# Token groups of two, three and three blocks, with the second group's front spread over the pairs of two blocks

## The chip, the core and the metric

The kernel runs on one core of one Trainium2 chip. The metric is device time in microseconds (us) of one execution; lower is better. Three runs of the kernel before gave 3722.76, 3727.45 and 3729.0 us, median 3727.45.

## The reference, cut to what matters

One step of a hybrid decoder layer for 1024 prompt tokens and 8 sample tokens, all in float32, model width 1024.

```python
n = rmsnorm(x, g_mix) * (1 + sc1) + sh1            # sc, sh, gt come from silu(c) @ w_ada + b_ada
z = n @ w_in                                       # 1024 -> 4096: a_lin, a_gate, u, v, g_a, g_b
a = silu(layernorm(causal_dwconv(a_lin * sigmoid(a_gate)))) @ w_conv_out      # 31 taps
b = (u * chunk_spatial_gate(layernorm(v))) @ w_gmlp_out                       # chunks of 128 tokens
x = x + gt1 * ((sigmoid(g_a) * a + sigmoid(g_b) * b) @ w_out)
n2 = rmsnorm(x, g_ffn) * (1 + sc2) + sh2
# PEER, per token: q = n2 @ w_q (8 heads x 2 halves), scores against 128 keys each,
# top 16 of both halves, top 16 of their sums -> 8 x 16 = 128 experts out of 16384
act = gelu(u_tab[eid] . n2);  x = x + gt2 * sum(softmax_weight * act * v_tab[eid])
y = rmsnorm(x, g_final)
```

Outputs are y for all tokens, the last 30 inputs of the convolution and the samples' v rows.

## The kernel before, in words

Tokens lie in eight blocks of 128 (block 8 is the eight samples). Everything up to the choice of experts, the **front** (`front`, one generator for each of TensorE, ScalarE and VectorE), works on a group of blocks: norm and transpose, gate and lin (line 505 with the helper `tiles`), u, v (line 561), spatial gate, branch B with w_gmlp_out, the mean and variance of the convolution, branch A with w_conv_out, the output projection (line 657), second norm, transposes back, queries (line 505), scores (line 697) with `top16` on VectorE, candidate tables, and the `route` of the group's first block (lines 1405 to 1446; lines 1429, 1432 and 1434 pick the expert numbers). G1 is block 0, G2 blocks 1 to 3, G3 blocks 4 to 7 and the samples. A matmul of the front takes a 128x128 weight tile and `tg` token columns: 128, 384, and twice 260. `ng` is the number of such column tiles. Float32 matmuls appear as two instructions each. The convolution is 124 operations of VectorE (line 1172) strewn between the other steps.

The weights don't stay on the chip. SP loads them anew for each group as 32 pieces of 1 MB into a ring of three (lines 386 and 387), each piece after the piece three before it is used up; the first front has the 24 pieces of w_ada between.

The experts are handled in **pairs** of slots. A pair is two gathers (GpSimd, line 1014), each of 128 rows of 8 KB: the u and v rows of one expert for each of 128 (token, slot) places. `PLAN` gives each pair one of three buffers, one of five from pair `WIDE_AT` = 256 on; a gather waits until the buffer's last pair has been used by TensorE (line 739). VectorE forms the products (line 1472) and, after the gelu on ScalarE (line 957), the masked weights (line 1489); TensorE adds the weighted v rows (line 739). A block has 64 pairs; with four pairs for the samples, put before the last block at pair 448, there are 516.

G1's front runs alone. The other fronts are woven in between the pairs by `beside_peer`: on each engine, for each pair, first `begin`, then so many steps of the front's generator, then extra work, then `finish` (on VectorE: products, front steps, route pieces, weights; on TensorE: front steps, then the pair's matmuls). How many steps a pair gets comes from `spread_front`: every step of a front has a weight (`front_weights`: 3 for a step with work, 1 or 2 for others), and the weights are spread evenly over a range of pairs, 0 to 59 for G2 (`END_B`) and 64 to 247 for G3 (`END_C`). At the last pair of its range an engine runs whatever is left of its generator. The remaining routes of a group run in pieces, one per pair, ten to a block (`routing_2`, `routing_3`, `extra`): those of G2 from pair 64 to 83, those of G3 at pairs 256, 320 and 384 and after, the samples' among them. GpSimd waits at a block's first pair for its route.

Of the kernel before, what the change touches and what calls it, by code (L numbers as in the profile page):

```python
# [20 lines left out]
D = 1024  # L21
NP = 1024
NS = 8
# [19 lines left out]
PIECE = 2048  # L43
NB1 = 4
GW = 520
QUAD = 32
NQ = P // QUAD
# [6 lines left out]
HEAVY = 3  # L54
END_B = 60
END_C = 4 * PAIRS - 8
WIDE_AT = 4 * PAIRS

# [57 lines left out]
def build(nc, t):  # L116
# [3 lines left out]
    with ctx:  # L120
# [13 lines left out]
        gt1_a = big[:, 6 * D:7 * D]  # L134
        sq_a = part(big, 7 * D, 1, D)
# [4 lines left out]
        AW = 512 + W - 1  # L140
        arena = sb("arena", [P, CC * (AW + 2 * GW) + 5 * DC])
        aT = part(arena, 0, CC, AW)
        yT = part(arena, CC * AW, CC, GW)
        v_tm = part(arena, CC * (AW + GW), 5, DC)
        uT = part(arena, CC * (AW + GW) + 5 * DC, CC, GW)
        ysq = part(arena, CC * (AW + GW), CC, GW)
        x_first = part(arena, CC * AW, 5, D)
        eq = part(arena, CC * AW + 5 * D, 2, TOP, NC)
        xn2 = part(arena, 3768, 5, D)
        xn1 = sb("xn1", [P, NB1, D])  # L150
        xr = sb("xr", [P, NQ, D])
        v16 = part(arena, 0, 5, NCH, TOP)
        i16f = part(arena, 5 * NCH * TOP, 5, NCH, TOP)
        i16 = i16f.bitcast(u32)
        rep = part(arena, 10 * NCH * TOP, 4, NKEY)

# [3 lines left out]
        sgt = part(w1, 1024, CC, P)  # L160
        rbc = w1[:, 2048:2048 + GW]
        xs = part(w1, 0, 2, D)
# [81 lines left out]
        def group(n, blocks, tg, xn, tables):  # L244
            g = Group()
            g.n, g.blocks, g.nb, g.tg, g.xn = n, blocks, len(blocks), tg, xn
            g.nt = sum(width(b) for b in blocks)
            g.ng = g.nt // tg
            g.nf = sum(b < NB for b in blocks)
            g.np = g.nf * P  # L250
            g.S = {k: S[f"{k}{1 if n < 3 else 2}"] for k in group_names}
            g.S |= {k: S[f"{k}{n}"] for k in ("x_in", "out_x1")}
            g.base = totals(G1) if n == 2 else {}

            g.order = list(range(g.nb)) if n < 3 else [0, 1, 2, 4, 3]
            g.cand = part(tables, 0, g.nb * H, NC)
            g.cid = part(tables, g.nb * H * NC, g.nb * H, NC)
            g.posf = part(mbuf, 3200, g.nb * H, TOP) if n < 3 else part(mbuf, 0, g.nb * H, TOP)
            g.crep = part(mbuf, 3200 + 512, H, NC) if n < 3 else part(mbuf, 1024, H, NC)
            g.eq = eq if n < 3 else part(mbuf, 2048, 2, TOP, NC)  # L260
            g.gt1 = (gt1_a, gt1_b, gt1_c)[n - 1]
            return g

        G1 = group(1, [0], P, xn1[:, 0:1, :], mbuf)
        G2 = group(2, [1, 2, 3], 3 * P, xn1[:, 1:4, :], mbuf)
        G3 = group(3, list(range(NB1, NBT)), 260, xn2, wring)
        GROUPS = (G1, G2, G3)
        before = {2: G1, 3: G2}

        def cols(b):  # L270
            i = 0 if b == 0 else b - 1 if b < NB1 else b - NB1
            return slice(i * P, i * P + width(b))
# [44 lines left out]
        def front_weights(g):  # L317

            for work, idle in ((4 * CC * g.ng, 5), (2 * CC * g.ng, 5), (4 * g.nb, 12), (2 * g.nb, 5),
                               (3 * KC * g.ng, 5), (2 * g.ng, 17), (3 * KC * g.ng, 7), (8 * g.nb, 3)):  # L320
                if work == 4 * CC * g.ng:
                    yield from norm_steps(g)
                    yield from [1] * 5
                yield from [HEAVY] * work
                yield from [1] * idle
            yield from norm_steps(g)
            yield from [1] * 5
            yield from [HEAVY] * (2 * g.nb)
            yield from [1] * 3
            yield from [HEAVY] * (NCH * (2 * g.ng + 1))  # L330
            yield from [1] * (2 * g.ng + 1) * 3
            yield from [1] * 4 + [2] * (36 if g.n == 3 else 20)

        def spread_front():

            steps = [(None, 0)] * NPAIRS
            for g, lo, hi in ((G2, 0, END_B), (G3, PAIRS, END_C)):
                weights = list(front_weights(g))
                total, spent, at = sum(weights), 0, 0
                for pair_ in range(lo, hi):  # L340
# [25 lines left out]
        def x1_again(b):  # L366
            return mbuf[:, b * D:(b + 1) * D] if b < NB1 else wring[:, (b - NB1) * D:(b - NB1 + 1) * D]

# [7 lines left out]
        def _(sp):  # L376
            for name, dst in (("cT", cT), ("bada", bada), ("gmix", gmix), ("gffn", gffn)):
                sp.dma_start(dst[:], t[name]).then_inc(S["c_in"], 16)
            sp.dma_start(xn1[:, 0, :], t["x"][0:P, :]).then_inc(S["x_in1"], 16)

# [51 lines left out]
            for n in range(first_piece[3] + 3, len(pieces)):  # L432
                if n == first_piece[3] + 11:
# [5 lines left out]
                    sp.wait_ge(*G3.to("v_done", G3.nb))  # L439
                    sp.dma_start(t["out_v"], v_tm[0:NS, 4, :]).then_inc(S["out_v"], 16)  # L440
                if n == first_wo + 2:
# [23 lines left out]
        def _(pe):  # L465
# [278 lines left out]
            def sample_x(k):  # L744
# [3 lines left out]
                for half in range(2):  # L748
                    mm = mmul(ps[:, pair(k) + half, :], ident[0:NS, k:k + 1].broadcast_to([NS, P]),  # L749
                              xn2[0:NS, 4, 512 * half:512 * (half + 1)], start=True, stop=True)  # L750
                mm.then_inc(S["xb_mm"], 1)
# [13 lines left out]
        def _(act_):  # L765
# [11 lines left out]
            def replicate(h, c):  # L777
# [3 lines left out]
                if c == 0:  # L781
                    g = G1 if b == 0 else G2 if b < NB1 else G3
                    act_.wait_ge(*g.to("n2_done", b - g.blocks[0] + 1))
# [7 lines left out]
            def front(g):  # L791
# [124 lines left out]
                for ch in range(NCH + 3):  # L916
                    yield from gap(2 * ng - 1)
                    if ch < NCH:
# [5 lines left out]
                        if g.n == 3:  # L924
                            last = ac(qs[:, ch, :], ps[:, 3 + 2 * (ch % 2), tg - NS:tg], ACT.Copy)
                        last.then_inc(s["q_done"], 1)
# [10 lines left out]

                yield from gap(27 if g.n == 3 else 11)
                next(g.numerators)
# [32 lines left out]

            exps = {PAIRS + ROUTE_PIECES * i + 6: G2 for i in range(2)}
            exps |= {at + 6: G3 for at in (4 * PAIRS, 5 * PAIRS, 6 * PAIRS, 6 * PAIRS + ROUTE_PIECES + 1)}
            copies = {half_start(h - 1) + 20 + c: (h, c) for h in range(2, 2 * NB) for c in range(8)}
# [18 lines left out]
        def _(pool):  # L994
# [22 lines left out]
            for at in range(NPAIRS):  # L1017
# [4 lines left out]
                elif b is None and m == 0:  # L1022
                    pool.wait_ge(S["idxs_ready"], 1)
                elif m == 0 and half == 0 and b < NB1:
                    pool.wait_ge(*G2.to("routes", b))
                elif m == 0 and half == 0:
                    pool.wait_ge(*G3.to("routes", b - NB1 + 1 if b < NB - 1 else G3.nb))
                if at == WIDE_AT:
# [13 lines left out]
        def _(dve):  # L1042
# [36 lines left out]
            def front(g):  # L1079
# [74 lines left out]
                else:  # L1154

                    link(v.tensor_tensor(conv_s, full_s[:], wdw[:].unsqueeze(2).broadcast_to([P, CC, NS, W]), ALU.mult))
                    link(v.tensor_reduce(yT[:, :, 512:GW], conv_s, AX.X, ALU.add))
                    v.tensor_tensor(yT[:, :, 512:GW], yT[:, :, 512:GW], cvec[:, 0, :].unsqueeze(2).broadcast_to([P, CC, NS]),
                                    ALU.add).then_inc(s["conv"], 1)
# [154 lines left out]
                if g.n == 3:  # L1314
                    dve.wait_ge(S["out_hist"], 16 * (1 + CC))
                    v.memset(v16[:, 4, :, :], 0.0)
                    link(v.memset(i16[:, 4, :, :], 0))

# [34 lines left out]
                if g.n == 3:  # L1353
                    dve.wait_ge(S["qs_mm"], 1)
                    for c in range(4):
                        dve.wait_ge(*g.to("s_done", NCH + c))
                        yield from top16([ps[0:NS, 2 + c, i * P:(i + 1) * P] for i in range(4)],
                                         [(4, 4 * c + i) for i in range(4)], NS, rep_s)
                    dve.wait_ge(*g.to("s_done", NCH + 4))
# [136 lines left out]
            def take_acc(n):  # L1496

                dve.wait_ge(S["rows_used"], ends[n] + 1)
                if n == 2 * (NB - 1):
                    out, acc, by = xn2[0:NS, 4, :], bank2(0)[0:NS, :], gts  # L1500
                else:
# [151 lines left out]
```

## Time and profile before

| | |
|---|---|
| median of three runs | 3727.45 us |
| profiled execution | 3729.06 us |
| its span, first to last instruction | 3727.5 us |
| mean granted clock of TensorE | 0.819 |
| busy: TensorE, VectorE, GpSimd, ScalarE | 2522.2, 2444.5, 1160.5, 592.7 us |
| moved by DMA | 1232.08 MB, 331 GB/s over the span |
| gathers / loads and stores | 1082.20 MB / 148.05 MB |

The span goes from the first to the last instruction. Busy times of engines overlap. A granted clock of 1.0 is 2.4 GHz, 0.5 is 1.2 GHz. The DMA share is the mean busy share of the core's 16 DMA engines. Matmuls are pipelined, so the busy time of TensorE holds some time in which it only drains.

### The profile page before, as it was taken

The numbers are of one execution on the slowest core, as the hardware profiler recorded it, in microseconds if no ns is written. First come the engines' busy times: TensorE is split into PE (matmuls) and PEld (weight loads), VectorE is DVE, ScalarE is ACT, GpSimd is POOL, SyncE is SP. The second block draws the span as 40 slices with busy tenths as digits, with TensorE's granted clock in tenths as the row PEclk, the third lists the DMA queues.
The fourth block names the chain that finished last, engine by engine and source line by source line (L and its number), as shares of the span: only waits on it lengthen the run. The fifth ranks groups of instructions, "written<-read, shape, count | busy, mean of one in ns | idle before, by whom it ended". The sixth has DMA issues, their size and how long they took to land. (4 is left out here: it accounts for less than half of the span.)

```text
span 3727.5 us, 28731 instructions
## 1 busy us (share of the span) xinstructions
PE 2522.2 (68%) x9500; PEld 1114.8 (30%) x9500; DVE 2444.5 (66%) x6272; ACT 592.7 (16%) x1135; POOL 1160.5 (31%) x1045
## 2 busy tenths in 40 slices
PE   6873888989467968779959953455555544566555
PEld 4553443455124525445525520000000000011000
DVE  1317486357887787554667897866776687656665
ACT  1013112211112114333020101010110101011100
POOL 0000121122123333323333322444444443444442
PEclk8986899989679979889979976777677776777677
DMA  6554566687567998889989986999999999998998
GB/s 210 219 198 158 203 259 239 237 308 297 227 253 296 366 319 334 337 327 360 404 358 403 387 316 249 378 422 422 421 369 421 421 381 370 422 422 326 423 421 336
DMA packets 183029, 1232.08 MB, mean 331 GB/s; under 512 B 29616, under 2 KB 30256, under 8 KB 35424
## 3 DMA queue, kind: packets, MB, share of 16 engines
q0 software_dynamic: 148608, 1082.20, 73.1%
q1 hardware_dynamic: 34272, 148.05, 10.5%
q8 instruction: 75, 1.23, 0.1%
q14 instruction: 74, 0.61, 0.0%
HBM read 1221.14 MB, written 9.02 MB: 330 GB/s over the span
## 5 line engine op out<-in xcount | busy, mean ns | idle before, releaser
L1014 POOL DMA_INDIRECT big<-in_experts,eid x920 | 1025.5, 1115 | 2316.9 <-PE ps L739 1809.2
L739 PE MATMUL ps<-big,wd 128*32 128x512 f32 x3680 | 1148.8, 757 | 763.8 <-DVE wd L1489 763.6
L1472 DVE SCALAR_TENSOR_TENSOR big<-big,xr 128x1024 f32<-128x1024 f32 x920 | 1116.6, 1223 | 683.1 <-DMA big<-in_experts,eid 681.7
L505 PE MATMUL ps<-big,wring 128*128 128x260 f32 (+2 forms) x2816 | 698.7, 403 | 133.2 <-issue 67.4
L739 PEld LDWEIGHTS ps<-big,wd 128*32 128x32 f32 x3680 | 202.5, 126 | 1568.2 <-DVE wd L1489 1112.3
L505 PEld LDWEIGHTS ps<-big,wring 128*128 128x128 f32 x2816 | 499.5, 202 | 367.8 <-issue 205.3
L957 ACT ACTIVATE gel<-act 128x2 f32<-128x2 f32 x516 | 104.9, 203 | 2541.7 <-DVE big L1472 2275.1
L1489 DVE TENSOR_SCALAR wd<-mask,gel,gate 128x32 f32<-128x32 f32 x1024 | 270.8, 350 | 77.2 <-ACT gel L957 70.1
L739 PE MATMUL ps<-w,wd 128*32 128x512 f32 x208 | 145.6, 841 | 125.8 <-DVE wd L1489 124.5
L1172 DVE SCALAR_TENSOR_TENSOR arena<-arena,wdw 128x128 f32<-128x128 f32 (+2 forms) x360 | 180.8, 566 | 0.0
L739 PE MATMUL ps<-arena,wd 128*32 128x512 f32 x208 | 145.6, 841 | 0.0
L657 PE MATMUL ps<-wring,mbuf 128*128 128x256 f32 (+1 forms) x576 | 132.4, 386 | 5.3 <-ACT w L901 2.2
L505 PE MATMUL ps<-arena,wring 128*128 128x260 f32 (+2 forms) x512 | 125.5, 389 | 0.0
L657 PEld LDWEIGHTS ps<-wring,mbuf 128*128 128x128 f32 (+1 forms) x576 | 101.4, 180 | 43.7 <-issue 18.0
L957 ACT ACT_TABLE_LOAD x83 | 106.5, 1283 | 1.3
L521 PE MATMUL ps<-ident,w 128*128 128x128 f32 (+1 forms) x144 | 27.4, 354 | 111.3 <-DVE w L1094 111.3
L1014 POOL DMA_INDIRECT w<-in_experts,eid x52 | 60.2, 1157 | 134.8 <-PE ps L739 128.6
L505 PEld LDWEIGHTS ps<-arena,wring 128*128 128x128 f32 x512 | 87.9, 193 | 40.9 <-issue 19.3
L1472 DVE SCALAR_TENSOR_TENSOR arena<-arena,xr 128x1024 f32<-128x1024 f32 x52 | 63.7, 1225 | 53.3 <-DMA arena<-in_experts,eid 53.3
L739 PEld LDWEIGHTS ps<-w,wd 128*32 128x32 f32 x208 | 23.3, 134 | 249.3 <-DVE wd L1489 195.5
L487 PE MATMUL ps<-wring,cT 128*9 128x256 f32 x384 | 89.9, 390 | 11.6 <-DMA wring<-in_w_ada 11.6
L1472 DVE SCALAR_TENSOR_TENSOR w<-w,xr 128x1024 f32<-128x1024 f32 x52 | 63.6, 1223 | 18.1 <-DMA w<-in_experts,eid 18.1
(200 smaller groups left out, 1875.2 us busy)
## 6 DMA issues: line engine op xcount, KB each, us to landing
wring<-in_w_in SPq DMA_DIRECT2D x48, 1024.0 KB
wring<-in_w_ada SPq DMA_DIRECT2D x24, 1024.0 KB
wring<-in_w_q SPq DMA_DIRECT2D x24, 1024.0 KB
big<-in_experts,eid POOLq DMA_INDIRECT x920, 17.5
wring<-in_w_out SPq DMA_DIRECT2D x12, 1024.0 KB
wring<-in_w_gmlp_out SPq DMA_DIRECT2D x6, 1024.0 KB
wring<-in_w_conv_out SPq DMA_DIRECT2D x6, 1024.0 KB
arena<-in_x SPq DMA_DIRECT2D x8, 512.0 KB
```

What stands on the lines that cost most here:

```text
L487: mm = mmul(ps[0:1 + NS, 7 * (i % 2), 0:256], cT[:, c, :], piece(ada_piece[i])[:, c, :], start=(c == 0), stop=(c == KC - 1))
L505: mm = mmul(out, piece(n)[:, c, col:col + P], src[:, c, gi * tg:(gi + 1) * tg], start=(c == 0), stop=(c == k - 1))
L521: mm = nc.tensor.transpose(bank2(pair(i))[:, c * P:c * P + w], xs[0:w, i % 2, c * P:(c + 1) * P], ident[0:w, 0:w])
L657: mm = mmul(ps[0:w, 2 + i % 6, 0:256], mT[:, c, cols(b)], piece(n + col)[:, c, :], start=(c == 0), stop=(c == KC - 1))
L739: mm = mmul(ps[QUAD * j:QUAD * (j + 1), h, :], wd[:, 2 * (at % 4) + jj, :], row(2 * slot + jj)[:, D + 512 * h:D + 512 * (h + 1)], start=(m ...
L957: ac(gel[:, c:c + 2], act[:, c:c + 2], ACT.Gelu).then_inc(S["gelu"], 1)
L1014: gp.indirect_dma_start(row(r), None, t["experts"], bass.IndirectOffsetOnAxis(ap=index, axis=0)).then_inc(s_row[r], 16)
L1172: ins = v.scalar_tensor_tensor(out=y, in0=aT[:, c, kk:kk + g.np], scalar=wdw[:, c, kk:kk + 1], in1=y, op0=ALU.mult, op1=ALU.add)
L1472: last = v.scalar_tensor_tensor(out=row(r)[:, 0:D], in0=row(r)[:, 0:D], scalar=1.0, in1=x, op0=ALU.mult, op1=ALU.mult, accum_out=act[:, c: ...
L1489: last = v.tensor_scalar(wd[:, c, :], mask[:], gel[:, c:c + 1], gate[:, b % 4, 2 * half + jj, m:m + 1], ALU.mult, ALU.mult)
```

## The change

The blocks are grouped anew: G1 is blocks 0 and 1 (256 columns), G2 blocks 2 to 4 (384), G3 blocks 5 to 7 and the samples (one tile of 392 columns in place of two of 260). `NBL`, `SB` and `GT` name G3's number of blocks, the samples' place in it and its width, and the buffers' offsets follow. G2's front is spread over pairs 0 to 123, G3's over pairs 128 to 311, the two further buffers open at pair 320. The second route of G1 runs in pieces at pairs 0 to 9; G2's routes run at pairs 128 to 147, G3's at 320, 384 and after. The rest of the diff replaces literals by these names.

```diff
--- before.py
+++ after.py
-NB1 = 4
+NB0 = 2
+NB1 = 5
+NBL = NBT - NB1
+SB = NBL - 1
+GT = (NBL - 1) * P + NS
 GW = 520
+AGAIN = 4
...
-END_B = 60
-END_C = 4 * PAIRS - 8
-WIDE_AT = 4 * PAIRS
+END_B = NB0 * PAIRS - 4
+END_C = NB1 * PAIRS - 8
+WIDE_AT = NB1 * PAIRS
...
-            g.order = list(range(g.nb)) if n < 3 else [0, 1, 2, 4, 3]
+            g.order = list(range(g.nb)) if n < 3 else [*range(SB - 1), SB, SB - 1]
...
-        G1 = group(1, [0], P, xn1[:, 0:1, :], mbuf)
-        G2 = group(2, [1, 2, 3], 3 * P, xn1[:, 1:4, :], mbuf)
-        G3 = group(3, list(range(NB1, NBT)), 260, xn2, wring)
+        G1 = group(1, list(range(NB0)), NB0 * P, xn1[:, 0:NB0, :], mbuf)
+        G2 = group(2, list(range(NB0, NB1)), (NB1 - NB0) * P, xn1[:, NB0:NB1, :], mbuf)
+        G3 = group(3, list(range(NB1, NBT)), GT, xn2, wring)
...
-            yield from [1] * 4 + [2] * (36 if g.n == 3 else 20)
+            yield from [1] * 4 + [2] * (28 if g.n == 3 else 20)
...
-            for g, lo, hi in ((G2, 0, END_B), (G3, PAIRS, END_C)):
+            for g, lo, hi in ((G2, 0, END_B), (G3, NB0 * PAIRS, END_C)):
...
-            sp.dma_start(xn1[:, 0, :], t["x"][0:P, :]).then_inc(S["x_in1"], 16)
+            for b in G1.blocks:
+                sp.dma_start(xn1[:, b, :], t["x"][b * P:(b + 1) * P, :]).then_inc(S["x_in1"], 16)
...
-                            last = ac(qs[:, ch, :], ps[:, 3 + 2 * (ch % 2), tg - NS:tg], ACT.Copy)
+                            last = ac(qs[:, ch, :], ps[:, 2 + 2 * (ch % 2), tg - NS:tg], ACT.Copy)
...
-                yield from gap(27 if g.n == 3 else 11)
+                yield from gap(19 if g.n == 3 else 11)
...
-            exps = {PAIRS + ROUTE_PIECES * i + 6: G2 for i in range(2)}
-            exps |= {at + 6: G3 for at in (4 * PAIRS, 5 * PAIRS, 6 * PAIRS, 6 * PAIRS + ROUTE_PIECES + 1)}
+            exps = {6: G1}
+            exps |= {NB0 * PAIRS + ROUTE_PIECES * i + 6: G2 for i in range(2)}
+            exps |= {at + 6: G3 for at in (5 * PAIRS, 6 * PAIRS, 6 * PAIRS + ROUTE_PIECES + 1)}
...
-                elif m == 0 and half == 0 and b < NB1:
-                    pool.wait_ge(*G2.to("routes", b))
-                elif m == 0 and half == 0:
-                    pool.wait_ge(*G3.to("routes", b - NB1 + 1 if b < NB - 1 else G3.nb))
+                elif m == 0 and half == 0 and b > 0:
+                    g = group_of(b)
+                    pool.wait_ge(*g.to("routes", b - g.blocks[0] + 1 if b < NB - 1 else G3.nb))
...
-                for i in range(1, 4):
+                for i in (1, 2):
                     yield from route(G3, i)
                 yield from to_slots()
-                yield from route(G3, 4)
-
-            second, third, norms = routing_2(), routing_3(), early_norm()
+                yield from route(G3, 3)
+
+            first, second, third, norms = route(G1, 1), routing_2(), routing_3(), early_norm()
             def extra(at):
-                if PAIRS <= at < PAIRS + 2 * ROUTE_PIECES:
+                if at < ROUTE_PIECES:
+                    next(first, None)
+                if NB0 * PAIRS <= at < NB0 * PAIRS + 2 * ROUTE_PIECES:
                     next(second, None)
-                for b, count in ((4, ROUTE_PIECES), (5, ROUTE_PIECES), (6, 2 * ROUTE_PIECES + 1)):
+                for b, count in ((5, ROUTE_PIECES), (6, 2 * ROUTE_PIECES + 1)):
```

`group_of(b)` returns the group of a block; the deleted chains of conditions in `replicate` and `cols` call it.

## Rows read from the trace of the kernel before

**Rows 1.** The page: slices of TensorE and the DMA engines, one DMA issue

```profile
PE   6873888989467968779959953455555544566555
...
DMA  6554566687567998889989986999999999998998
...
wring<-in_w_in SPq DMA_DIRECT2D x48, 1024.0 KB
```

**Rows 2.** Stages: us; PE, PEld, DVE, ACT, POOL busy (instructions); clock; DMA share; GB/s

```profile
0.00:365.00 365.00, 242.05 (x1472) 179.16 (x1472) 134.82 (x527) 58.58 (x108) 10.23 (x19) 0.84 0.55 200
365.00:1030.00 665.00, 526.86 (x1850) 274.08 (x1852) 417.99 (x1182) 120.25 (x190) 132.00 (x126) 0.88 0.66 251
1030.00:2293.00 1263.00, 960.69 (x3996) 525.99 (x3992) 927.95 (x2484) 271.26 (x474) 406.91 (x369) 0.87 0.87 336
2293.00:3693.00 1400.00, 776.93 (x2146) 133.12 (x2148) 947.14 (x2050) 139.18 (x355) 611.39 (x532) 0.74 0.97 401
3693.00:3727.50 34.50, 15.65 (x40) 2.41 (x36) 16.57 (x33) 3.45 (x8) 0.00 (x0) 0.65 0.46 190
```

**Rows 3.** Line 1472 by the third front's phases, four instructions a pair

```profile
1030.00:1210.00 180.00, 53.11 (x88) 0.82 0.71 269
1210.00:1389.00 179.00, 63.38 (x104) 0.86 0.95 346
1389.00:1545.50 156.50, 58.76 (x96) 0.95 0.91 343
1545.50:1764.00 218.50, 74.46 (x121) 0.89 0.86 333
1764.00:1866.30 102.30, 43.64 (x72) 0.98 1.00 404
1866.30:1946.00 79.70, 28.16 (x46) 0.69 0.87 354
1946.00:2179.50 233.50, 98.79 (x161) 0.98 0.98 389
2179.50:2292.90 113.40, 29.05 (x50) 0.65 0.65 242
2334.00:2664.00 330.00, 156.69 (x256) 0.75 0.99 409
```

**Rows 4.** Busy time in a stretch of stage D with no route

```profile
2950.00:3000.00 50.00, 27.55 (x80) 4.50 (x76) 31.03 (x68) 7.44 (x16) 24.26 (x21) 0.76 1.01 422
```

**Rows 5.** Timeline of TensorE: start us, us, operation, count

```profile
285.53 1.95 PE L505 MATMUL ps<-big,wring 128*128 128x128 f32 x16
...
899.55 5.33 PE L505 MATMUL ps<-big,wring 128*128 128x384 f32 x16
...
1600.32 1.92 PE L505 MATMUL ps<-big,wring 128*128 128x260 f32 x8
1602.16 1.91 PE L739 MATMUL ps<-big,wd 128*32 128x512 f32 x8
```

**Rows 6.** Windows of stage A: gate to u, branch B, queries

```profile
58.30:93.60 35.30, 27.16 (x192) 26.46 (x192) 9.77 (x37) 3.50 (x9) 0.00 (x0) 0.82 0.44 164
138.80:169.20 30.40, 22.96 (x171) 22.80 (x172) 20.92 (x82) 1.94 (x7) 0.00 (x0) 0.83 0.26 104
277.30:314.30 37.00, 35.17 (x288) 34.80 (x288) 22.74 (x115) 6.60 (x20) 0.00 (x0) 0.93 0.61 212
```

**Rows 7.** Timeline of VectorE in a route; windows of the gathers' line 1014

```profile
992.73 1.82 DVE L1432 TENSOR_TENSOR arena<-arena,mbuf 128x1600 f32<-128x1600 f32 x1
...
990.00:1013.00 23.00, 0.00 (x0) 0.50 0.00 0
2265.00:2290.00 25.00, 2.39 (x2) 0.50 0.24 84
```

**Rows 8.** Windows in stage C where weights or a chain are late

```profile
1465.00:1490.00 25.00, 18.72 (x70) 12.05 (x72) 12.50 (x22) 3.36 (x5) 3.75 (x4) 0.76 0.69 272
1565.00:1590.00 25.00, 11.49 (x34) 4.76 (x32) 15.27 (x21) 10.30 (x13) 3.75 (x4) 0.70 0.54 204
```

More of the change, by code:

```diff
@@ L134, in build @@
         gt1_a = big[:, 6 * D:7 * D]
-        sq_a = part(big, 7 * D, 1, D)
+        sq_a = part(big, 7 * D, NB0, D)
         mbuf = sb("mbuf", [P, KC * GW])
@@ L138, in build @@
         wring = sb("wring", [P, RING * PIECE])
-        AW = 512 + W - 1
-        arena = sb("arena", [P, CC * (AW + 2 * GW) + 5 * DC])
+        AW = (NBL - 1) * P + W - 1
+        arena = sb("arena", [P, CC * (AW + 2 * GT) + 5 * DC])
         aT = part(arena, 0, CC, AW)
[L143 to L149, printed above, removed]
+        yT = part(arena, CC * AW, CC, GT)
+        v_tm = part(arena, CC * (AW + GT), NBL, DC)
+        uT = part(arena, CC * (AW + GT) + 5 * DC, CC, GT)
+        ysq = part(arena, CC * (AW + GT), CC, GT)
+        x_first = part(arena, CC * AW, NBL, D)
+        eq = part(arena, CC * AW + NBL * D, 2, TOP, NC)
+        xn2 = part(arena, CC * (AW + 2 * GT) + 5 * DC - NBL * D, NBL, D)
         xn1 = sb("xn1", [P, NB1, D])
         xr = sb("xr", [P, NQ, D])
-        v16 = part(arena, 0, 5, NCH, TOP)
-        i16f = part(arena, 5 * NCH * TOP, 5, NCH, TOP)
+        v16 = part(arena, 0, NBL, NCH, TOP)
+        i16f = part(arena, NBL * NCH * TOP, NBL, NCH, TOP)
         i16 = i16f.bitcast(u32)
-        rep = part(arena, 10 * NCH * TOP, 4, NKEY)
+        rep = part(arena, 2 * NBL * NCH * TOP, 4, NKEY)
         w1 = sb("w1", [P, 3 * D])
@@ L160, in build @@
         sgt = part(w1, 1024, CC, P)
-        rbc = w1[:, 2048:2048 + GW]
+        rbc = w1[:, 2048:2048 + GT]
         xs = part(w1, 0, 2, D)
@@ L262, in group, with group_of @@
             return g
-        G1 = group(1, [0], P, xn1[:, 0:1, :], mbuf)
-        G2 = group(2, [1, 2, 3], 3 * P, xn1[:, 1:4, :], mbuf)
-        G3 = group(3, list(range(NB1, NBT)), 260, xn2, wring)
+        G1 = group(1, list(range(NB0)), NB0 * P, xn1[:, 0:NB0, :], mbuf)
+        G2 = group(2, list(range(NB0, NB1)), (NB1 - NB0) * P, xn1[:, NB0:NB1, :], mbuf)
+        G3 = group(3, list(range(NB1, NBT)), GT, xn2, wring)
         GROUPS = (G1, G2, G3)
         before = {2: G1, 3: G2}
+        def group_of(b):
+            return G1 if b < NB0 else G2 if b < NB1 else G3
         def cols(b):
-            i = 0 if b == 0 else b - 1 if b < NB1 else b - NB1
+            i = b - group_of(b).blocks[0]
             return slice(i * P, i * P + width(b))
@@ L366, in x1_again @@
         def x1_again(b):
-            return mbuf[:, b * D:(b + 1) * D] if b < NB1 else wring[:, (b - NB1) * D:(b - NB1 + 1) * D]
+            return mbuf[:, b * D:(b + 1) * D] if b < AGAIN else wring[:, (b - AGAIN) * D:(b - AGAIN + 1) * D]
         gfin = wring[:, 5 * D:6 * D]
@@ L439, in _ @@
                     sp.wait_ge(*G3.to("v_done", G3.nb))
-                    sp.dma_start(t["out_v"], v_tm[0:NS, 4, :]).then_inc(S["out_v"], 16)
+                    sp.dma_start(t["out_v"], v_tm[0:NS, SB, :]).then_inc(S["out_v"], 16)
                 if n == first_wo + 2:
@@ L749, in sample_x @@
                     mm = mmul(ps[:, pair(k) + half, :], ident[0:NS, k:k + 1].broadcast_to([NS, P]),
-                              xn2[0:NS, 4, 512 * half:512 * (half + 1)], start=True, stop=True)
+                              xn2[0:NS, SB, 512 * half:512 * (half + 1)], start=True, stop=True)
                 mm.then_inc(S["xb_mm"], 1)
@@ L781, in replicate @@
                 if c == 0:
-                    g = G1 if b == 0 else G2 if b < NB1 else G3
+                    g = group_of(b)
                     act_.wait_ge(*g.to("n2_done", b - g.blocks[0] + 1))
@@ L1023, in _ @@
                     pool.wait_ge(S["idxs_ready"], 1)
-                elif m == 0 and half == 0 and b < NB1:
-                    pool.wait_ge(*G2.to("routes", b))
-                elif m == 0 and half == 0:
-                    pool.wait_ge(*G3.to("routes", b - NB1 + 1 if b < NB - 1 else G3.nb))
+                elif m == 0 and half == 0 and b > 0:
+                    g = group_of(b)
+                    pool.wait_ge(*g.to("routes", b - g.blocks[0] + 1 if b < NB - 1 else G3.nb))
                 if at == WIDE_AT:
@@ L1156, in front @@
                     link(v.tensor_tensor(conv_s, full_s[:], wdw[:].unsqueeze(2).broadcast_to([P, CC, NS, W]), ALU.mult))
-                    link(v.tensor_reduce(yT[:, :, 512:GW], conv_s, AX.X, ALU.add))
-                    v.tensor_tensor(yT[:, :, 512:GW], yT[:, :, 512:GW], cvec[:, 0, :].unsqueeze(2).broadcast_to([P, CC, NS]),
+                    link(v.tensor_reduce(yT[:, :, g.np:GT], conv_s, AX.X, ALU.add))
+                    v.tensor_tensor(yT[:, :, g.np:GT], yT[:, :, g.np:GT], cvec[:, 0, :].unsqueeze(2).broadcast_to([P, CC, NS]),
                                     ALU.add).then_inc(s["conv"], 1)
@@ L1315, in front @@
                     dve.wait_ge(S["out_hist"], 16 * (1 + CC))
-                    v.memset(v16[:, 4, :, :], 0.0)
-                    link(v.memset(i16[:, 4, :, :], 0))
+                    v.memset(v16[:, SB, :, :], 0.0)
+                    link(v.memset(i16[:, SB, :, :], 0))
                 def top16(scores, out, w, reps):
@@ L1357, in front @@
                         yield from top16([ps[0:NS, 2 + c, i * P:(i + 1) * P] for i in range(4)],
-                                         [(4, 4 * c + i) for i in range(4)], NS, rep_s)
+                                         [(SB, 4 * c + i) for i in range(4)], NS, rep_s)
                     dve.wait_ge(*g.to("s_done", NCH + 4))
@@ L1499, in take_acc @@
                 if n == 2 * (NB - 1):
-                    out, acc, by = xn2[0:NS, 4, :], bank2(0)[0:NS, :], gts
+                    out, acc, by = xn2[0:NS, SB, :], bank2(0)[0:NS, :], gts
                 else:
```

## The prediction

> **What bounds the kernel now.** I read the page's slices first [rows 1]: TensorE is busiest in the first two thirds, and the DMA engines are full only in the last 40%. So the kernel has stages with different limits. I placed them by the row products of line 1472, four instructions for each pair of expert slots (two products, two accumulator reads), and so by pair number. Then I asked each stage for its busy times [rows 2]. Stage A, the first group's front alone, runs to 365.0 us with the DMA engines 0.55 busy. Stage B, pairs 0 to 63 beside the second group's front, takes 665.0 us: TensorE 526.86, DMA 0.66. Stage C, pairs 64 to 247 beside the third group's front, takes 1263.0 us: DMA 0.87, VectorE 927.95. Stage D, pairs 248 to 515 and the sample pairs, takes 1400.0 us at a DMA share of 0.97. A tail of 34.5 follows. Sum 3727.5, the span; the profiled execution took 3729.06, 1.6 above the median of the three runs, 3727.45.
>
> What a pair costs when nothing else is in the way is seen in [rows 4]: share 1.01 at 422 GB/s. A pair gathers 2 x 128 rows of 8 KB, 2.10 MB, hence 4.97 us. A group's 32 weight pieces of 1 MB (those of w_in, 48 for three groups, in [rows 1]) are 33.5 MB, 79.5 us at that rate. So the **DMA floor** of B is 64 x 4.97 + 80 = 398, and 267 us are lost; that of C is 184 x 4.97 + 80 = 994, and 269 are lost. D has 268 x 4.97 = 1332 and loses 68. The floor binds C and D nearly; B is bound by TensorE and by chains of dependent steps. In B the front's weight is 679 over 60 pairs, 11.3 a pair; in C 1151 over 184, 6.3.
>
> **The change, part by part.** *TensorE's work as a whole stays.* In all, 1032 columns pass each weight tile before and after (128+384+520; 256+384+392). Sixteen matmuls take 1.95 us at 128 columns and 5.33 at 384, eight take 1.92 at 260 [rows 5]: 13.2 ns per column and sixteen. So the third group's single tile of 392 costs what its columns cost, no less than two tiles of 260 for the same width, and the first group's 256 cost 3.64 for sixteen, 1.69 more than now. The weight loads lie beside the matmuls and cost nothing; were that cover gone, the narrow first stage would show it, and it has 179.16 us of them under 242.05 of matmuls [rows 2].
>
> Here a page speaks otherwise. The Trainium skill, "TensorE: Matmul & The Clock Gate", section "Back-to-back issue gap", gives sustained spacings of about 81 ns at 128 columns and 131 ns at 512 for pairs of load and matmul, so that wide tiles come nearly free. The rows show a matmul's time nearly in proportion to its columns; the measurement decides, and what the page's rule would give is the third rival.
>
> *Stage A grows.* Its windows [rows 6] give the terms. Gate, lin and u: 192 matmuls, 12 x 1.69 = 20, less some 5 of the 8 us of idle TensorE in that window, since weights have longer to arrive: 15. v: 32 more matmuls of 256 columns, 6. Spatial gate: 3. Branch B: 192 matmuls less the window's edge, 21, with the convolution's 20.92 us of VectorE still beneath. Mean and variance: 2, most of it under the ada matmuls. Branch A: 21. Output projection: 64 matmuls of 256 columns, 14. Second norm: another block's square, transposes, scale and copy, 7. Queries: 256 matmuls, 27, and 3 for the scores of a second block; VectorE's top16 of two blocks stays below TensorE's time. Candidate tables twice as wide 2.5, one more x load 1.5. Sum **+123**, so the first product stands at **488**. The range of this term is 475 (more DMA waits go) to 505 (none goes and the DVE chains add up).
>
> *Stage B' is pairs 0 to 127 beside the second group's front, 679 over 124 pairs, 5.5 a pair.* I cost it by phases, since the same phases stand in C [rows 3], where weight per pair is nearest. Per work unit of four contraction steps, TensorE takes 2.6 us at 384 columns against 1.8 at 260, so per pair in tile phases 1.83 x 2.6 = 4.7 against 2.09 x 1.8 = 3.7, both plus 1.9 for the pair's own eight matmuls [rows 5]. Pairs 0 to 14, norm and gate, beside the first group's second route (10 pieces, four of them three operations of 1.82 us [rows 7]): C's first 22 pairs took 180.0, 8.2 each, so 125. Pairs 15 to 32, u, v and spatial gate, at C's 6.9: 124. Pairs 33 to 46, branch B: C has 156.5 for 24 pairs, 6.5, plus 1 for the heavier tiles: 108. Pairs 47 to 65, mean and branch A: C has 218.5 for 29, of which 59 over the floor; with one column tile in place of two, so half the handovers between engines, I take 36 over a floor of 109: 145. Pairs 66 to 79, output projection, at the DMA floor as in C: 82. Pairs 80 to 87, norm and transposes: floor 40, and 20 of C's 25 above it, 60. Pairs 88 to 115, queries: floor 159 plus C's excess of 10, rounded, 171. Pairs 116 to 127, tables and route: between the floor of 60 and the 113.4 of C's tail, nearer to the latter because VectorE's chain sets both, less the samples' candidate lists: 92. **Sum 907**, or 191 over the floor of 716. The routing burst that the last front pair flushes now stops the pairs: the DMA engines stand still from 990 to 1013, at a quarter of their rate from 2265 to 2290 [rows 7]. It goes from 9 steps to 6 and stays a stall of some 24.
>
> *Stage C' is pairs 128 to 311 beside the third group's front, 753 over 184, 4.1 a pair.* Floor again 994. Against C's phases: norm and gate with two routes (21 pairs) 166, u/v/spatial gate (29) 184, branch B (19) 123, mean and branch A (25) 184, output projection (24) 131, norm and transposes (14) 88, queries (38) 213, tail (14) 116. **Sum 1205**, 58 under C's 1263. Most of C's loss is in fixed chains and bursts (start 60, u/v/sg 40, branch A 59, tail 53), which stay; only the tile phases thin out.
>
> *Stage D' is 64 pairs shorter*: pairs 312 to 515. C's pairs 256 to 319, with a route among them, took 330.0 [rows 3]; 1400 - 330 = **1070**. The fifth buffer's start moves along (pair 256 to 320). Tail 34.5.
>
> Pieces on the queues: SP issues the same 96 group pieces, one x load moves from the third to the first group; POOL issues the same gathers, the first one 123 us later and their waits on the routes moved with the blocks. ScalarE has one exponential moved into pair 6 with a table load, under the pairs.
>
> **Sum**: 488 + 907 + 1205 + 1070 + 34.5 = 3704.5 of span, 23 less than now; 3706 as an execution, **3703** against the median. Where the gain comes from: pairs 0 to 127 took 1132 (665 and the first 64 of C, at 7.3 each, 467) and should take 907; 123 of those 225 are paid in A, and the third front, later and on pairs that now ran at D's pace, pays back another 79.
>
> **The rivals.** *Thinner fronts hide better.* If the loss in B' and C' falls with the weight per pair (B' 267 x 5.5/11.3 = 130, C' 269 x 4.1/6.3 = 176) the sum is 61 + 35 lower, **3607**. For it: B with 11.3 and C with 6.3 lose the same over a third of the pairs and the whole. Against: the loss sits in bursts. Halfway, 3655, is likelier than the end.
>
> *Slower: the front's time adds to the pairs'.* TensorE takes its queue in order, only three pairs' rows are on hand, and a gather starts only when a pair's value matmuls are done; a wait for weights or for a VectorE chain in the front so stops the gathers (windows of 25 us at DMA shares of 0.54 and 0.69 in C, [rows 8]). Time over the pairs' own 4.97 is 347 in B and 349 in C, so it may be a constant of a front. Then B' = 636 + 347 = 983, C' = 914 + 340 = 1254, and all is **3829**. It decides from the point where B' and C' together lose over 432 us over their floors instead of my 402; now both lose 536. Against: the constant includes B's TensorE limit, which goes. Half of it gives 3766.
>
> *Wide tiles are cheap.* Were the narrow tiles bound by their weight loads, sixteen matmuls of 256 columns would take the 1.95 us of today, and A would grow by 52 x 1.69 = 88 less: **3615**. The times in [rows 5] speak against it. (By the page's two spacings, an estimate, sixteen would take about 2.4, and A would grow by some 65 less.)
>
> *It does not spread what it should.* The steps are spread evenly, but their waits are not: if a sixth of the 225 won in pairs 0 to 127 stays behind in chains and route bursts, the result is about even, **3727** to 3740.
>
> **How the numbers follow.** Forecast's case, 3665 to 3740: 0.48 (0.38 faster, 0.08 within, 0.02 slower). Thinner fronts, 3607 to 3665: 0.20, and wide tiles, 3615 to 3640, 0.02, all faster. Constant front, 3750 and up: 0.22. No spread: 0.08 (0.05 within, 0.03 slower). About 0.2%, 7.5 us, is what a measurement here can tell from no change. Faster 0.60, within 0.13, slower 0.27. The range 3645 to 3770 leaves out about one in ten at each end: the full constant above, the proportional loss below. With the bounds of A alone it would be 3690 to 3720.
>
> **What would show it.** First product at about 488; pair 128 at about 1395; pair 312 near 2600; 24 to 34 us holes of the gathers at pairs 123 and 311; sixteen first-group matmuls in 3.6 us; the third group's in 5.4. Wrong if pair 128 comes after 1430 (the constant) or before 1350, or if pairs 128 to 311 take over 1250.

## The result, and the profile after

The change made the kernel slower: 3813.25 us median of four runs (3798.04 to 3818.43) against 3726.52, a ratio of 1.0227 with a 95% interval of 1.0196 to 1.0257. The forecast was 3703, the range 3645 to 3770. The profiled execution took 3818.43, its span is 3816.7. One of the ten executions of e6 below ran in a slower state, at 5114.4 us, and is left out of its median.

First the page, its slices of TensorE and of the DMA engines, against [rows 1]. The second line now is full earlier, and has dips in the middle (7, 7, 6, 7) that it did not have.

```profile
PE   6888469777968736876777758853555554557554
...
DMA  5543359887999877896977999896999999998998
```

Then the stages by windows: us, PE, PEld, DVE, ACT and POOL busy with their instructions, granted clock, DMA share, GB/s. They answer to [rows 2], with pairs 0 to 127 as B' and 128 to 311 as C'.

```profile
0.00:481.80 481.80, 354.32 (x1632) 263.26 (x1632) 192.25 (x688) 67.14 (x114) 10.22 (x19) 0.90 0.42 154
481.80:1416.40 934.60, 693.14 (x2362) 304.09 (x2364) 639.16 (x1682) 157.34 (x277) 289.92 (x254) 0.86 0.83 322
1416.40:2711.50 1295.10, 892.58 (x2990) 346.99 (x2988) 873.38 (x2293) 197.64 (x379) 412.85 (x369) 0.83 0.84 325
2711.50:3782.00 1070.50, 595.65 (x1632) 103.00 (x1628) 719.20 (x1547) 106.53 (x273) 464.64 (x404) 0.74 0.98 400
3782.00:3816.70 34.70, 15.92 (x40) 2.60 (x40) 17.14 (x35) 3.61 (x9) 1.67 (x2) 0.65 0.48 199
```

| stage | forecast | measured |
|---|---|---|
| A, first front alone | 488 | 481.8 |
| B', pairs 0 to 127 | 907 | 934.6 |
| C', pairs 128 to 311 | 1205 | 1295.1 |
| D' and tail | 1104.5 | 1105.2 |

Of the miss of 112 us in the span, 90 stand in C' and 28 in B'; A gave 6 back. C' is 32 us longer than the old C [rows 2, third line] although it has the same 184 pairs, a quarter fewer columns, less TensorE time (893 against 961 us) and less VectorE time (873 against 928). No engine was short of time there; the pairs were held up. By C's phases [rows 3], now line 1481 with four instructions a pair, the windows are those of norm/gate/u, v/spatial gate, branch B, mean with branch A, and output projection:

```profile
1416.40:1631.00 214.60, 67.69 (x112) 0.83 0.79 305
1631.00:1795.70 164.70, 53.49 (x89) 0.82 0.82 294
1795.70:1932.00 136.30, 46.49 (x76) 0.82 0.87 338
1932.00:2132.70 200.70, 61.42 (x100) 0.87 0.79 311
2132.70:2278.90 146.20, 58.99 (x97) 0.82 0.93 372
```

I had set these windows where the list of weights, as I had read it, puts the phases. The mean and branch A took 200.7 for 25 pairs. The timeline of TensorE told why (start us, us, operation): inside that window the tile matmuls, line 514, come in long runs between the pairs' own, line 748.

```profile
1977.32 1.91 PE L748 MATMUL ps<-big,wd 128*32 128x512 f32 x8
1979.16 5.53 PE L514 MATMUL ps<-big,wring 128*128 128x392 f32 x16
1984.53 2.80 PE L514 MATMUL ps<-arena,wring 128*128 128x392 f32 x8
1994.66 8.22 PE L514 MATMUL ps<-big,wring 128*128 128x392 f32 x16 [7.34 <-issue]
2002.81 1.91 PE L748 MATMUL ps<-big,wd 128*32 128x512 f32 x8
2004.65 2.90 PE L514 MATMUL ps<-arena,wring 128*128 128x392 f32 x8
2007.39 5.43 PE L514 MATMUL ps<-big,wring 128*128 128x392 f32 x16
2012.66 2.80 PE L514 MATMUL ps<-arena,wring 128*128 128x392 f32 x8
2015.38 1.91 PE L748 MATMUL ps<-big,wd 128*32 128x512 f32 x8
```

Five steps of eight matmuls stand between two pairs, then four; the list as I had read it gives one or two. All 192 matmuls of branch A ran from 1947.0 to 2035.3, 24 steps in 88 us, and the pairs had 58 of line 748 in that time, seven pairs:

```profile
1947.00:2035.30 88.30, 68.26 (x192) 37.04 (x192) 0.94 0.62 235
```

```profile
1947.00:2035.30 88.30, 13.41 (x58) 2.68 (x60) 0.94 0.62 235
```

(Windows of line 514 and of line 748 in that stretch. The DMA engines fall to a share of 0.62.) That is over three steps a pair where 4.1 of weight a pair should give 1.4. So the list is not what I had taken it for. `front_weights` puts the norm's light entries in front of the phase it recognises by `if work == 4 * CC * g.ng`. For the new third group, with four blocks and one column tile, the gate phase has 4 x 4 x 1 = 16 steps, and the v phase has 4 x nb = 16 as well. The norm's entries, 24 of them with a weight of 32, enter the list twice, and from v on, each phase of real steps falls partly on entries meant for idle ones: v at 2.7 steps a pair, branch B at 2.4, branch A at 3.0, and the front's steps run out at pair 300, before its range ends at 311. With five blocks and two tiles (20 and 32) or three blocks and one (12 and 16) the condition holds once.

### The profile page after: what moved, and what is told of

Same layout as the page of the kernel before. It is cut to its first block and busy times, and to the rows that moved or that the text cites. A ratio compares the mean times of both kernels' runs of the same rounds, so it can differ in the third digit from the quotient of the medians.

```text
span 3816.7 us, 26875 instructions
## 1 busy us (share of the span) xinstructions
PE 2551.6 (67%) x8652; PEld 1019.9 (27%) x8652; DVE 2441.1 (64%) x6243; ACT 532.3 (14%) x1050; POOL 1179.3 (31%) x1045
## 5 line engine op out<-in xcount | busy, mean ns | idle before, releaser
L1024 POOL DMA_INDIRECT big<-in_experts,eid x948 | 1076.6, 1136 | 2426.4 <-PE ps L748 1809.4
L748 PE MATMUL ps<-big,wd 128*32 128x512 f32 x3792 | 1213.4, 775 | 911.3 <-DVE wd L1498 909.4
L514 PE MATMUL ps<-big,wring 128*128 128x256 f32 (+2 forms) x2112 | 679.8, 475 | 111.5 <-issue 57.0
L514 PEld LDWEIGHTS ps<-big,wring 128*128 128x128 f32 x2112 | 407.8, 199 | 404.5 <-issue 205.0
L1181 DVE SCALAR_TENSOR_TENSOR arena<-arena,wdw 128x384 f32<-128x384 f32 (+1 forms) x360 | 180.3, 568 | 0.0
L748 PE MATMUL ps<-w,wd 128*32 128x512 f32 x152 | 107.7, 850 | 85.3 <-DVE wd L1498 85.3
L514 PE MATMUL ps<-arena,wring 128*128 128x256 f32 (+2 forms) x384 | 120.4, 456 | 0.0
L796 ACT ACTIVATE xr<-xn 32x1024 f32<-32x1024 f32 x80 | 84.2, 1053 | 1.7
L706 PE MATMUL ps<-keys,w 128*128 128x128 f32 x256 | 45.3, 319 | 54.6 <-DVE arena L1346 54.6
L1481 DVE DVE_READ_ACCUMULATOR big<-big,xr 128x1 f32 x948 | 77.8, 82 | 0.0
```

The lines of the kernel that those rows point to most:

```text
L514: mm = mmul(out, piece(n)[:, c, col:col + P], src[:, c, gi * tg:(gi + 1) * tg], start=(c == 0), stop=(c == k - 1))
L706: mm = mmul(ps[:, 6 + k % 2, i * P:(i + 1) * P], qbuf[:, k % 2, i * P:(i + 1) * P], keys[:, k % 2, :], start=True, stop=True)
L748: mm = mmul(ps[QUAD * j:QUAD * (j + 1), h, :], wd[:, 2 * (at % 4) + jj, :], row(2 * slot + jj)[:, D + 512 * h:D + 512 * (h + 1)], start=(m ...
L796: made = ac(xr[QUAD * q:QUAD * (q + 1), j, :], xn[QUAD * j:QUAD * (j + 1), :], ACT.Copy)
L1024: gp.indirect_dma_start(row(r), None, t["experts"], bass.IndirectOffsetOnAxis(ap=index, axis=0)).then_inc(s_row[r], 16)
L1181: ins = v.scalar_tensor_tensor(out=y, in0=aT[:, c, kk:kk + g.np], scalar=wdw[:, c, kk:kk + 1], in1=y, op0=ALU.mult, op1=ALU.add)
```

## The experiments

Each changes the kernel named. Stages are taken from the profiled execution, ratios against the kernel before from the same chip. There were three chips, on which the kernel before had medians of 3727.0 (e1 to e4), 3724.3 (e5 to e8) and 3729.2 us (e9 and e10); where a difference of medians crosses them, the one by the ratios is given too.

**e1: the changed kernel, its list of weights put right.**

```diff
-            for work, idle in ((4 * CC * g.ng, 5), ...
+            for k, (work, idle) in enumerate(((4 * CC * g.ng, 5), ...
-                if work == 4 * CC * g.ng:
+                if k == 0:
```

> Theory M: in the list of step weights the norm's light entries are put in wherever a phase has 4*CC*ng steps. With four blocks and one column tile the v phase has 4*nb = 16 = 4*CC*ng steps, so 32 entries of norm and gap stand a second time in the third front's list, and every later phase of real work falls on entries meant for another (branch A's 24 steps in 8 pairs). With the entries put in once, stage C' (pairs 128 to 311) falls from 1295 us to about 1210, the median from 3813 to 3725 (3700 to 3745). Rival K: a front costs a constant whatever its spread; then C' stays at 1280 to 1300 and the time at 3795 to 3820.

(The 32 there is the entries' weight.) Measured: 3760.26 us, ratio 1.0089 (1.0069 to 1.0108), 53 under the changed kernel. Windows of line 1481, from v/spatial gate to the output projection, in the same order as above:

```profile
1621.30:1762.80 141.50, 53.68 (x88) 0.81 0.95 345
1762.80:1894.00 131.20, 46.69 (x76) 0.92 0.91 348
1894.00:2062.00 168.00, 61.46 (x100) 0.86 0.91 351
2062.00:2195.20 133.20, 59.27 (x97) 0.94 1.00 408
```

v and spatial gate are 23 us shorter, mean and branch A 33, and C' as a whole 1237.6 against 1295.1. The 192 matmuls of branch A now stand in a window with 160 of line 748, 20 pairs:

```profile
1925.00:2062.00 137.00, 40.66 (x160) 7.72 (x160) 0.89 0.91 349
```

B' is 930.2, as before within 5. Theory M holds and rival K is out, but the gain is 53 where I had expected 88, and the time lies above the range expected: C' stays 33 over my 1205, so something else is in it. By the same windows the queries take the most of it, 248.6 us for the 213 of the prediction.

**e4: the kernel before, with the same fault put in.**

```diff
-                if work == 4 * CC * g.ng:
+                if work == 4 * CC * g.ng or (g.n == 3 and work == 4 * g.nb):
```

> The kernel before, with the same second set of norm entries put into the third front's list (37 more light entries at the v phase, where it has 20 steps). Theory M: stage C (pairs 64 to 247) goes from 1263 us to 1310 to 1350 and the time to 3775 to 3815. Rival K: C stays within 15 us, the time at 3727.

Measured: 3773.29, ratio 1.0117 (1.0097 to 1.0137). Here the entries are 27, their weight is the 37 named. Its stages B and C:

```profile
362.70:1025.90 663.20, 522.10 (x1850) 271.71 (x1852) 418.04 (x1183) 120.31 (x190) 140.32 (x126) 0.89 0.66 252
1025.90:2339.00 1313.10, 975.11 (x3998) 529.20 (x3996) 927.86 (x2483) 255.67 (x462) 413.42 (x369) 0.86 0.84 321
```

B is untouched and C goes from 1263.0 to 1313.1, with TensorE's and VectorE's busy times within 15 us of those in [rows 2]. By the medians the fault costs 46 us here and 53 in the changed kernel, by nothing but the place of the steps. The median came out 2 us below the range expected.

**e2: as e1, the third group's 392 columns in two tiles of 196.**

```diff
-        G3 = group(3, list(range(NB1, NBT)), GT, xn2, wring)
+        G3 = group(3, list(range(NB1, NBT)), GT // 2, xn2, wring)
...
-            yield from [1] * 4 + [2] * (28 if g.n == 3 else 20)
+            yield from [1] * 4 + [2] * (36 if g.n == 3 else 20)
```

(and the sample columns' PSUM bank and one gap that follow from it)

> As the run before, with the third group's 392 columns as two tiles of 196, so each step is half as long and there are twice as many. Theory T: one tile of 392 makes lumps of work between pairs that the three buffers can't cover; then C' is 30 to 60 us under that of the weights put right, the median near 3680. Theory M alone: within 15 us of the weights put right, since the columns are the same. Rival K: no change from 3813.

Measured: 3719.53, ratio 0.9978 (0.9957 to 0.9998), 41 under e1. B' and C':

```profile
483.80:1419.20 935.40, 692.41 (x2362) 303.24 (x2364) 638.91 (x1681) 157.44 (x277) 288.02 (x254) 0.86 0.83 322
1419.20:2620.40 1201.20, 858.96 (x3836) 471.09 (x3832) 873.95 (x2321) 260.20 (x466) 417.16 (x369) 0.86 0.90 352
```

C' is 1201.2 where my phases had summed to 1205. TensorE's time is the same as e1's within 9 us, with 848 more instructions, and C' falls by 36, inside theory T's 30 to 60. So a single tile has a price of 41 us though its columns cost no more. The median is above the 3680 named because e1's was too.

That it is the length of a step, as theory T says, is not shown, because the edit changes three things. The steps are half as long. They also fill more of the range: the list has 292 steps of weight 3 in place of 186 beside nearly the same light entries, so branch A's columns go to 24 pairs and not 17. And steps that wait for each other stand further apart (`top16`, for one, has `ng` - 1 idle steps between its parts). Windows of the pairs' products over branch A's steps, in the kernel before (two tiles of 260), e1 and e2 (four instructions a pair):

```profile
1588.90:1738.90 150.00, 56.52 (x92) 0.93 0.87 331
1925.10:2039.70 114.60, 41.84 (x68) 0.92 0.89 335
1951.30:2087.60 136.30, 59.01 (x97) 0.94 0.95 384
```

A pair took 6.5, 6.7 and 5.7 us, with about 540, 550 and 390 columns a pair (its steps times their width). So with about equal columns the step of 260 gains little over the one of 392, and the thinner spread seems to give most. The larger gain is in the queries. Their window in e1 and in e2, 38 pairs each, and the wait of TensorE's score matmuls (line 706) for `top16` on VectorE (line 1346) in it (us, times, longest), in the same order:

```profile
2283.70:2532.30 248.60, 92.93 (x152) 0.89 0.88 348
2285.40:2506.70 221.30, 93.33 (x152) 0.95 0.97 389
```

```profile
PE ps L706 <- DVE arena L1346: 30.8, 12, 5.5
PE ps L706 <- DVE arena L1346: 0.8, 1, 0.8
```

With one tile TensorE stands in its queue until VectorE's chain is through, with the pairs' matmuls behind it. How the 41 us divide among the three no run tells.

**e5: as e2, and the second group in two tiles of 192.**

```diff
-        G2 = group(2, list(range(NB0, NB1)), (NB1 - NB0) * P, xn1[:, NB0:NB1, :], mbuf)
+        G2 = group(2, list(range(NB0, NB1)), (NB1 - NB0) * P // 2, xn1[:, NB0:NB1, :], mbuf)
```

> As the third group in two tiles of 196, and the second group's 384 columns as two tiles of 192 too. Theory T (long steps between pairs stall the three buffers): stage B' (pairs 0 to 127) falls from 935 us to 895 to 915 and the median from 3719.5 to 3680 to 3700. If the tile's length does nothing in B' (its loss is in chains and route bursts), B' stays within 10 and the time at 3719.

Measured: 3697.84, ratio 0.9933 (0.9916 to 0.9949): faster than the kernel before and 115 us under the changed one.

```profile
481.50:1390.00 908.50, 685.33 (x3212) 429.38 (x3214) 640.91 (x1711) 211.47 (x357) 290.22 (x254) 0.87 0.85 331
```

B' is 908.5, my forecast 907; C' stays at 1202.0. Against e2 that is 22 us by the medians, 17 by the ratios. As in e2, the second front's work also fills more pairs, branch A 18 in place of 13. The grouping is 0.7% faster than the kernel before when both fronts run in two tiles.

**e6: the kernel before, its second group in two tiles of 192.**

```diff
-        G2 = group(2, [1, 2, 3], 3 * P, xn1[:, 1:4, :], mbuf)
+        G2 = group(2, [1, 2, 3], 3 * P // 2, xn1[:, 1:4, :], mbuf)
```

> The kernel before, its second group's 384 columns as two tiles of 192. Stage B there has 3.8 tile steps a pair and TensorE full in them, so theory T expects little: B from 665 to 645 to 660, the time 3727 to 3707 to 3722. If long steps cost wherever they stand, 40 us or more, as the third group's two tiles gave.

Measured: 3733.66, the median of nine executions, ratio 1.0025 (1.0014 to 1.0037), and B 671.7 against 665.0. Neither branch of the expectation came. In stage B, where TensorE was busy 527 of the 665 us, two tiles gave nothing. There the score matmuls of the kernel before had waited only 3.3 us for `top16`, so this run fits the last of e2's three changes as well as theory T. The profiled execution took 3743.23, 10 over the median, so the 7 us more in B can't be told from that.

**e3: as e1, the second front over pairs 0 to 91.**

```diff
-END_B = NB0 * PAIRS - 4
+END_B = 92
```

> As the weights put right, with the second front over pairs 0 to 91 in place of 0 to 123. Rival K (the front's time adds to the pairs'): pairs 0 to 127 keep their 935 us within 15, the time equals that of the weights put right. Spreading hides work: those pairs take 970 to 1000 us and the time grows by 35 to 65.

Measured: 3793.87, ratio 1.0173 (1.0154 to 1.0192), 34 over e1; pairs 0 to 127 took 964.7 against 930.2. Both lie just short of the range given for spreading. The spread hides work, by 34 us for the last quarter of its range: the additive rival is out. A loss proportional to the weight per pair would have grown from 214 over the floor of 716 to 289, and it grew to 249, so thinning helps less than in proportion too.

**e7 and e8: is it the three buffers?** e7 is e2 without the copies to `xr`; `gt2` stands in the products in their place, so expert activations are not the step's. e8 gives the memory won to a fourth pair buffer below pair 320.

```diff
-        xr = sb("xr", [P, NQ, D])
...
-                made = ac(xr[QUAD * q:QUAD * (q + 1), j, :], xn[QUAD * j:QUAD * (j + 1), :], ACT.Copy)
...
-                    x = xr[:, 2 * half + jj, :]
+                    x = gt2[:]
```

```diff
-        free = range(3 if at < WIDE_AT else 5)
+        free = (0, 1, 2, 5) if at < WIDE_AT else range(5)
...
+        more = sb("more", [P, 4 * D])
```

> Control for the next run: the third group in two tiles, with the copies of the tokens' rows to xr left out and gt2 in their place in the products, so the output is not the step's. ScalarE loses some 140 copies of 1.05 us that stand between its gelus. If they hold up gelus, 10 to 30 us are gained; otherwise the time stays at 3719 within 8.

> As the run before, with the 16 KB won given to a fourth pair buffer for all pairs before 320. Theory S: in B' and C' a pair waits because only three pairs' rows are in turnaround, so every front step between landing and use takes gather time away; with four, B' falls from 935 to 850 to 890 and C' from 1201 to 1080 to 1140, the time by 110 to 200 against the run before. If the fronts' loss is in TensorE's and VectorE's own time or in the weight pieces, both stay within 30.

Measured: e7 3727.06, ratio 1.0006 (0.9991 to 1.0021), so leaving out the copies gains nothing (8 us more than e2 by the medians). e8 3562.85, ratio 0.9569 (0.9553 to 0.9585), 164 under e7. B' and C' of e7, then of e8:

```profile
479.60:1412.90 933.30, 689.48 (x2362) 301.05 (x2364) 639.87 (x1681) 132.39 (x253) 288.61 (x254) 0.86 0.83 323
1412.90:2620.90 1208.00, 859.53 (x3836) 467.16 (x3832) 874.68 (x2321) 214.23 (x422) 419.39 (x369) 0.86 0.90 350
```

```profile
481.80:1345.50 863.70, 675.54 (x2362) 299.83 (x2364) 636.00 (x1681) 132.28 (x253) 292.07 (x254) 0.88 0.87 346
1345.50:2464.30 1118.80, 837.46 (x3836) 463.21 (x3832) 870.43 (x2322) 214.36 (x422) 413.73 (x368) 0.87 0.94 380
```

The waits in C' (who waited for whom: us, times, longest) of e7, then of e8:

```profile
POOL big L1015 <- PE ps L747: 686.7, 177, 17.8
...
DVE big L1470 <- DMA big<-in_experts,eid: 301.4, 217, 6.1
```

```profile
POOL big L1016 <- PE ps L748: 471.6, 132, 17.2
...
POOL more L1016 <- PE ps L748: 140.5, 44, 14.3
...
DVE big L1471 <- DMA big<-in_experts,eid: 172.7, 131, 4.2
DVE more L1471 <- DMA more<-in_experts,eid: 43.5, 44, 2.5
```

In e8 the fourth buffer is `more` and has rows of its own. With them, GpSimd waits 612.1 us for a free buffer, 75 less, and VectorE 216.2 for rows, 85 less, while TensorE is busy 22 us less in C' and VectorE 4. Theory S holds: the time, B' and C' all lie in its ranges, and its rival's 30 us are far off. It names what the two faults act on. A buffer is in turnaround from the issue of its gather to the pair's last matmul; every front step between landing and use lengthens that, and with three buffers the DMA engines then run out of gathers.

**e9: the changed kernel itself, with e7's and e8's edits.** Its list and its tile of 392 stay as they are; the edits are those above.

> The changed kernel itself, its list of weights and its long tiles unmended, with the copies to xr left out (gt2 in the products, output not the step's) and a fourth pair buffer for pairs below 320. Against the same two edits on the two-tile kernel (3562.9) the unmended list and tile cost 53 + 41 = 94 us with three buffers. Theory S: a fourth buffer covers part of the lumps, so they cost 30 to 70 here, the time 3595 to 3635, C' 1150 to 1190. If the lumps cost TensorE's own time, all 94 stay: 3650 to 3665.

Measured: 3616.35, ratio 0.9701 (0.9676 to 0.9726). The two faults, 94 us with three buffers (3813.25 to 3719.53), cost 53 with four (3616.35 against 3562.85; 49 by the ratios). C' is 1170.9, in its range. The fourth buffer covers some 41 us of lumps, as S has it, not all.

**e10: as e5, the weight pieces of the second and third group an eighth as wide.** The fronts of these groups then compute on stale weights.

```diff
+                w = PIECE if n < first_piece[2] else 256
-                sp.dma_start(wring[:, (n % RING) * PIECE:(n % RING + 1) * PIECE], src[col])...
+                sp.dma_start(wring[:, (n % RING) * PIECE:(n % RING) * PIECE + w], src[col][:, 0:w])...
```

> As both groups in two tiles, with the weight pieces of the second and third group loaded at an eighth of their width, 64 x 0.92 MB less (139 us at 422 GB/s), so the output is not the step's; TensorE's work, the waits and the order stay. If the weights' bytes and their late arrival set the fronts' loss, B' falls by 60 to 90 and C' by 70 to 100, the time to 3530 to 3570. Theory S (turnaround of three buffers is what binds, and the pieces fill DMA time that would stand idle): the time falls by less than 80, to above 3618.

Measured: 3618.55, ratio 0.9702 (0.9678 to 0.9726), 79 under e5 by the medians, 86 by the ratios; B' 880.9, C' 1165.0, so 28 and 37 less, in a profiled execution 17.5 us over the median. That lies on or just over the edge of theory S's 80 and far short of the other expectation: of 139 us of transfer 79 to 86 come back. So theory S's word that the pieces fill time in which the DMA engines would stand idle is right for under half of them. The bytes of the weights do cost time, and they are the smaller part: B' and C' of e5 are 560 us over the 312 pairs' own 4.97 each.

## Why the prediction was wrong

*TensorE's cost per column: right.* Sixteen matmuls of 256 columns took 3.62 us (3.64 forecast), sixteen of 392 5.43 (5.4). The timeline of the changed kernel in stage A:

```profile
377.22 3.62 PE L514 MATMUL ps<-big,wring 128*128 128x256 f32 x16
```

By the sustained spacings of the Trainium skill, "TensorE: Matmul & The Clock Gate", section "Back-to-back issue gap", about 81 ns at 128 columns and 131 at 512, sixteen of 256 would take about 2.4, an estimate. The trace does not agree for these float32 matmuls; that rival is out.

*Stage A grew by 117, forecast 123; stage D' came out at 1070.5, forecast 1070.* Both sums held; the single terms of A were not measured.

*Stage B': 934.6 for 907.* The step that failed is "with one column tile in place of two, so half the handovers between engines, I take 36 over a floor of 109", and with it the whole practice of costing B' from C's phases by columns alone. C had two tiles of 260. By the prediction's own pairs, mean and branch A took 157.3 us where it has 145, and the queries 191.9 where it has 171; the other phases together came out 6 under. With two tiles of 192 the two phases took 139.8 and 165.6, and B' 908.5. In the queries TensorE's score matmuls had waited 25.0 us for `top16`; with two tiles in both fronts they waited 1.3 in all of B'. What I had counted as a saving, one tile with fewer handovers, was the loss, 17 to 22 us. That the 908.5 then meets 907 is in part luck: output projection and tail were 13 over each, and five other phases 4 to 6 under each.

*Stage C': 1295.1 for 1205.* Two steps failed. "753 over 184, 4.1 a pair": the list weighs 785 and has the norm's entries twice. I had read the condition in `front_weights` as the name of the first phase and had not put the new group's numbers into it; two seconds of arithmetic, 4 x 4 x 1 against 4 x 4, would have shown it. It cost 53 us (e1). And again the single tile, 41 us (e2), most of it in the queries. The two make 94, and C' with both mended is 1201. This sum too holds partly because its errors cancel: by its own windows mean and branch A took 160.6 for 184, the output projection 141.2 for 131, the queries 221.3 for 213. Of the signs given, "pairs 128 to 311 take over 1250" came true; pair 128 came at 1416.4, before the 1430 that was to mark the constant.

*The rivals.* My slower rival, at 3829 the nearest to the result in its number, is not what happened: its constant front is refuted by e1 and e3. It had the mechanism half right: only three pairs' rows on hand, gathers that start only when a pair is done, and waits for a VectorE chain that stop them. e8 shows that this is what the loss acts on. It was missing why one form of the front should suffer more than another. "It does not spread what it should" was the right heading, at a chance of 0.08 and a price of 24 to 37 us; I gave it chains and bursts as the cause and not the list itself. "Thinner fronts hide better" is true with a weaker slope than the one I worked out, as far as one run tells (e3).

*The routing burst* at the last pair of the second front's range I put at a stall of some 24. In the changed kernel GpSimd, the issuer of the gathers, waited 23.8 us there; pair 123 starts at 1369.0 and pair 124 at 1395.5:

```profile
1399.57 1.03 POOL L1024 DMA_INDIRECT big<-in_experts,eid  x1 [23.79 <-PE ps L748]
```

At pair 311 no such hole came: the longest wait of GpSimd between 2660 and 2730 was 4.9 us, since the third front's steps had run out by then. In e1, with the list put right, it is there, again 23.8 us.

## What to carry to other kernels

Where a schedule is made from numbers, evaluate its conditions for the new sizes before costing anything: a comparison that stands for "the first phase" held for two phases once a group had four blocks and one tile. Where work is slipped between the turns of a ring of few buffers, try it in shorter steps even if their sum stays the same: here it was worth 41 us in one front and about 20 in another, and nothing where TensorE was busiest. Look then at what else the cut changed: how many turns share the work, and how far apart two steps stand that wait for each other. And when three theories speak of a stall around a ring, one more buffer in a kernel that leaves something out is the cheapest way to tell.

## What I had not expected

The DMA engines were 0.83 to 0.90 busy in B' and C', which I had taken to leave little to win. A fourth buffer took them only to 0.87 and 0.94 (e7 and e8) and that alone was 164 us, 70 in B' and 89 in C'. A mean share near 0.9 over a stage of a millisecond hid holes that were worth 4% of the kernel.
